# A last projection turned over: token blocks stationary, 512 output channels moving, and a LayerNorm that follows the tokens

## The chip, the cores and the metric

One core of one Trainium2 chip runs the program. The metric is the device time of the whole kernel in microseconds; lower is better. TensorE multiplies a stationary 128 x 128 block by columns that move past it, VectorE (DVE), ScalarE (ACT) and GpSimd (POOL) work on rows of 128 partitions, SyncE (SP) issues most transfers. The engines run on their own and meet at semaphores.

## What is computed

Two layers over T = 384 tokens (128 context, 256 latent) of D = 2048 channels. The second, odd layer is the one that matters here:

```python
def odd_mixer(h, w_in, conv_w, conv_b, ln_g, ln_b, w_out):
    a, b, g = jnp.split(h @ w_in, 3, axis=-1)
    u = a * jax.nn.sigmoid(b)
    u = dwconv(u, conv_w) + conv_b
    u = jax.nn.silu(layernorm(u, ln_g, ln_b))
    return (u * jax.nn.silu(g)) @ w_out
...
        y_p = layernorm(ALPHA * y_p + gt_c * o_p, ln_g[l], ln_b[l])
        y_s = layernorm(ALPHA * y_s + gt_s * o_s, ln_g[l], ln_b[l])
```

The input of w_out has 4096 channels (KE = 32 blocks of 128), its output 2048 (KD = 16 blocks). The gate gt is a vector over channels, one for context and one for latent tokens.

## The kernel before

Everything lies with channels on the partitions and the 384 tokens in the free dimension. Float32 accuracy comes from three products: each operand is split into a high part (fp32r) and the remainder, and high x high, high x low and low x high are added up in PSUM. The weights come as slabs of 8 blocks of 128 x 128 (512 KB): SP loads a slab into one of four raw buffers, ScalarE copies it to w_hi, and VectorE (even slabs) or GpSimd (odd slabs) subtracts to w_lo. Rings of four slabs tie the engines together: w_hi of slab k + 4 waits for slab k to be used. Engines work in order and by hand-written program: a "pair" is two slabs.

The phases follow each other: FIRST and EVEN (the even layer's input projection with attention), OUT0 (its output projection), ODD (the odd layer's input projection, 192 slabs or 96 pairs, with the convolution on VectorE), OUT1 (the last output projection, 4 bodies of 16 slabs), and the final LayerNorm with the stores.

In OUT1 a body makes four strips of 128 output channels x 384 tokens, one in each of the banks 0 to 3; a slab serves one strip. The weight block is stationary and the 384 tokens of o_hi or o_lo move. As each strip ends, VectorE multiplies it by the gate (a scalar for each partition) and adds it to the scaled x, less a pivot; ScalarE squares it, GpSimd adds up sum and squares over the blocks. Behind the last matmul `token_moments` sums over the partitions with ones on TensorE, VectorE and ScalarE make mean and root, TensorE spreads them, and `normalise_output` centres, scales and (with ScalarE's `affine`) applies gain and bias, block by block; SP stores 16 blocks of 192 KB.

In the last steps of ODD and the first of OUT1 the mixed activations o are still being made (NORM and SPLIT in `odd_step`: VectorE subtracts and scales, ScalarE applies SiLU, GpSimd multiplies by the gate path, ScalarE and VectorE split into o_hi and o_lo). ScalarE's `gate_out` evicts the last gate strips of ODD from the banks 2 and 3 at the start of its OUT1 part. The bank waits of TensorE and of ScalarE's eviction are these:

```python
                if t0 == 0:
                    if q == 0 and not (ph is FIRST and s in (CG_, XIN_)):
                        pe.wait_ge(bank_free[b], value)
                    pe.wait_ge(lo_ready[odd], ready)
...
                        if first and layer and not pair:
                            for s, (_, c) in odd_ready(PAIRS_ODD):
                                gate_out(s, c)
```

## Time and profile before

| | us |
|---|---|
| time, median of 3 runs | 2566.84 (2565.62 to 2566.97) |
| span of the profiled execution | 2565.9 |
| TensorE busy in it | 2515.2 |
| VectorE, ScalarE, GpSimd busy | 1959.0, 934.7, 922.9 |

The time is that of unprofiled runs. The profile has one execution of its own, whose span runs from the first to the last instruction; what lies around the span is not in it. Matmul records overlap: a matmul of 384 columns has a record of some 334 ns, and the next one starts much earlier. What a matmul costs in a stream is read from start to start.

### The profile page before, as it was taken

To read this page: it belongs to the slowest core of one execution; us is meant where nothing else is said; L and a number is where in the kernel's file an instruction comes from. 1 tells how busy PE (TensorE), PEld (TensorE's weight loads), DVE (VectorE), ACT (ScalarE), POOL (GpSimd) and SP (SyncE) were. 2 spreads that over 40 slices of the span, in tenths; PEclk is the share of its full clock that TensorE was granted. 3 is DMA by queue.
4 is the path that set the end of the run, shared out by engine and by line. 5 is a ranking of instruction groups with operands and counts; after the bars stand their busy time and mean duration, and the time that the engine had idled before them with its cause. 6 is when DMAs were issued, how large, how long until landed. Compare 5 with 4: busy or idle time off the path is not lost.

```text
span 2565.9 us, 40433 instructions
## 1 busy us (share of the span) xinstructions
PE 2515.2 (98%) x14486; PEld 2467.1 (96%) x14486; DVE 1959.0 (76%) x3411; ACT 934.7 (36%) x1232; POOL 922.9 (36%) x618
## 2 busy tenths in 40 slices
PE   6999999999999999999999999999999999999997
PEld 3699999999999999999999999999999999999997
DVE  2488888989888888889643389999999999484213
ACT  1233333333333333334322354333333333463223
POOL 0111111110111111111344566666666666572444
PEclk9999999999999999999999999999999999999998
DMA  9975666555565556565444334444343443564332
GB/s 387 347 214 189 200 193 198 184 195 197 193 209 195 191 184 199 189 200 161 155 147 139 129 111 136 138 138 130 126 137 129 135 129 130 180 208 131 124 125 89
DMA packets 131567, 442.02 MB, mean 172 GB/s; under 512 B 16720, under 2 KB 27216, under 8 KB 131456
## 3 DMA queue, kind: packets, MB, share of 16 engines
q1 hardware_dynamic: 114912, 409.23, 46.8%
q0 software_dynamic: 7328, 18.71, 3.6%
q10 hardware_dynamic: 9216, 12.59, 1.5%
q8 instruction: 70, 1.15, 0.2%
q14 instruction: 41, 0.34, 0.0%
HBM read 423.03 MB, written 15.18 MB: 171 GB/s over the span
## 4 chain that ended last, share of the span: by engine, by line
PE 90%; DVE 5%; DMA 3%; issue 1%; ACT 1%; POOL 1%; SPq 0%; ACTq 0%; DVEq 0%; POOLq 0%
PE bank L508 29%; PE bank L510 29%; PE bank L509 29%; DMA map<-in_w_ada_dram 2%; DVE w_lo L404 1%; PE bank L607 1%; PE bank L524 1%; DMA raw<-in_w_ada_dram 1%; DVE vk L1127 1%; DVE x L1317 0%; DVE part L1032 0%; ACT w_hi L725 0%; DVE o_lo L1176 0%; POOL w_lo L404 0%; DVE probT L1149 0%
## 5 line engine op out<-in xcount | busy, mean ns | idle before, releaser
L508 PE MATMUL bank<-h_hi,w_hi 128*128 128x384 f32 x3543 | 1191.9, 336 | 4.9 <-DVE h_lo L970 2.3
L510 PE MATMUL bank<-h_hi,w_lo 128*128 128x384 f32 x3543 | 1184.6, 334 | 0.0
L509 PE MATMUL bank<-h_lo,w_hi 128*128 128x384 f32 x3543 | 1184.3, 334 | 0.0
L725 ACT ACTIVATE w_hi<-raw 128x1024 fp32r<-128x1024 f32 x572 | 595.4, 1058 | 867.7 <-PE bank L510 611.4
L404 POOL TENSOR_TENSOR w_lo<-raw,w_hi 128x1024 fp32r<-128x1024 f32 x247 | 603.8, 2462 | 544.6 <-ACT w_hi L725 542.3
L508 PEld LDWEIGHTS bank<-h_hi,w_hi 128*128 128x128 f32 x3543 | 665.6, 188 | 22.8 <-issue 12.6
L509 PEld LDWEIGHTS bank<-h_lo,w_hi 128*128 128x128 f32 x3543 | 665.7, 188 | 0.6
L510 PEld LDWEIGHTS bank<-h_hi,w_lo 128*128 128x128 f32 x3543 | 665.5, 188 | 0.0
L404 DVE TENSOR_TENSOR w_lo<-raw,w_hi 128x1024 fp32r<-128x1024 f32 x325 | 396.4, 1236 | 257.9 <-ACT w_hi L725 244.8
L1393 DVE SCALAR_TENSOR_TENSOR bank<-up,cw,bank 128x399 f32<-128x399 f32 x896 | 487.0, 627 | 0.0
L508 PE MATMUL bank<-o_hi,w_hi 128*128 128x384 f32 x1024 | 343.1, 335 | 1.7 <-DVE w_lo L404 1.0
L510 PE MATMUL bank<-o_hi,w_lo 128*128 128x384 f32 x1024 | 342.1, 334 | 0.0
L509 PE MATMUL bank<-o_lo,w_hi 128*128 128x384 f32 x1024 | 342.1, 334 | 0.0
L1032 DVE SCALAR_TENSOR_TENSOR part<-raw,cond,part 128x512 f32<-128x512 f32 x450 | 309.3, 748 | 38.0 <-DMA raw<-in_w_ada_dram 38.0
L508 PEld LDWEIGHTS bank<-o_hi,w_hi 128*128 128x128 f32 x1024 | 192.2, 188 | 3.3 <-DVE w_lo L404 1.4
L509 PEld LDWEIGHTS bank<-o_lo,w_hi 128*128 128x128 f32 x1024 | 192.3, 188 | 0.3
L510 PEld LDWEIGHTS bank<-o_hi,w_lo 128*128 128x128 f32 x1024 | 192.2, 188 | 0.0
L1482 POOL DMA_DIRECT2D part<-part x30 | 25.1, 836 | 335.1 <-DVE part L1032 239.9
L1492 POOL DMA_DIRECT2D out_new_v_dram<-vk x16 | 9.2, 576 | 325.3 <-DVE k_lo L1111 325.3
L1241 DVE SCALAR_TENSOR_TENSOR x<-bank,mod,x 128x256 f32<-128x256 f32 x64 | 23.8, 413 | 110.8 <-PE bank L510 110.8
L1149 DVE STREAM_TRANSPOSE probT<-prob 32x224 f32<-32x224 f32 x256 | 103.2, 403 | 3.8
L1390 DVE SCALAR_TENSOR_TENSOR bank<-up,cw,pivot 128x128 f32<-128x128 f32 x64 | 102.5, 1645 | 0.0
(188 smaller groups left out, 1526.5 us busy)
## 6 DMA issues: line engine op xcount, KB each, us to landing
raw<-in_w_in_even_dram SPq DMA_DIRECT2D x256, 512.0 KB, 4.2
raw<-in_w_in_odd_dram SPq DMA_DIRECT2D x192, 512.0 KB, 3.3
raw<-in_w_ada_dram SPq DMA_DIRECT2D x120, 512.0 KB, 4.2
map<-in_w_ada_dram SPq DMA_DIRECT2D x64, 512.0 KB, 13.5
raw<-in_w_out_even_dram SPq DMA_DIRECT2D x64, 512.0 KB, 3.9
raw<-in_w_out_odd_dram SPq DMA_DIRECT2D x64, 512.0 KB, 3.3
gates<-sg ACTq DMA_DIRECT2D x32, 192.0 KB, 1.9
lg<-gates ACTq DMA_DIRECT2D x32, 192.0 KB, 3.8
```

Of the source, the lines that this page charges most:

```text
L404: eng.tensor_tensor(w_lo[mine][:], raw[slot][:], w_hi[mine][:].bitcast(F32), ALU.subtract)\
L508: pe.matmul(out, w_hi[slot][:, t, :], hi[:, kk, :], start=(kk == 0), stop=False)
L509: pe.matmul(out, w_hi[slot][:, t, :], lo[:, kk, :], start=False, stop=False)
L510: mm = pe.matmul(out, w_lo[slot][:, t, :], hi[:, kk, :], start=False, stop=last)
L524: mm = pe.matmul(bank[B_S1][32 * g:32 * g + 32, 0:CHUNK], cond[:, kk, :], maps[n % MAP_RING][:, g % 2, :], start=(q == 0), stop=(q == PART ...
L607: mm = pe.matmul(bank[B_V][:, TC:T].rearrange("p (a b) -> p a b", a=2), v, probT[:, j:j + 4:3, :], start=(j == 0), stop=(j == 2))
L725: act.activation(w_hi[mine][:], raw[slot][:], ACT.Copy).then_inc(hi_ready, 1)
L1032: ins = dve.scalar_tensor_tensor(to, w, by, to, ALU.mult, ALU.add)
L1127: ins = dve.transpose(vk[t:t + 32, :, c:c + 32], values[c:c + 32, :, t:t + 32])
L1149: ins = dve.transpose(probT[k:k + 32, :, q:q + 32], tiles[q:q + 32, :, k:k + 32])
L1390: ins = dve.scalar_tensor_tensor(a[:, a0 + z:b0 + z], src[:, a0 + z:b0 + z], wt, pivot[:, a0:b0], ALU.mult, ALU.subtract)
L1393: ins = dve.scalar_tensor_tensor(a, src, wt, a, ALU.mult, ALU.add)
```

## The change

The last output projection swaps its operands. A block of 128 tokens of o_hi or o_lo is stationary, and 512 output channels of w_hi or w_lo move past it; a body makes the three token tiles of 128 x 512 of a chunk of 512 channels, in the banks 0, 1, 2 or 3, 5, 6 in turn. A slab now holds two blocks of 128 input channels (halves) x 512 outputs. For each half the three products follow each other, each going over the three token tiles. Only the last four slabs of the last body run tile by tile, so that tile 0 is complete before tile 1. x itself must lie with tokens on the partitions: in ODD, TensorE transposes it block by block and ScalarE copies it back scaled by ALPHA. The gate becomes a row over channels, which needs two small transfers of the gate from SBUF to DRAM and a broadcast back; gain and bias come as broadcast rows too. The final LayerNorm uses bn_stats for each chunk and tile, and SP stores twelve pieces of 256 KB in the output's own layout. The pivot, the sums and squares of this layer and the former tail go.

```diff
+TILE_BANKS = ((0, 1, 2), (3, 5, 6))
+BY_TILE = OUT1.nw - RING
...
+        def tile_chunk(i, n):
+            return x[:, 4 * i:4 * i + 4, n * P:(n + 1) * P]
...
-                for r, (_, s, _) in enumerate(OUT1.order):
-                    load(OUT1, i, r, slab_of(OUT1, r, w_out_odd, i * 4 + s))
...
-                sp.dma_start(yT[:, t, :], x[:, t, :]).then_inc(y_stored, 16)
...
+                for r in range(OUT1.nraw):
+                    load(OUT1, i, r, w_out_odd[ds(i, 1), r].rearrange("s p f -> (s p) f"))
+            for n in range(TILES):
+                for i in range(OUT1.bodies):
+                    if i < SHIFTED_BY_DVE:
+                        sp.wait_ge(applied, n * SHIFTED_BY_DVE + i + 1)
+                    else:
+                        sp.wait_ge(applied_last, n + 1)
+                    sp.dma_start(y[n * P:(n + 1) * P, i * WIDE:(i + 1) * WIDE].rearrange("p (a b) -> p a b", b=P),
+                                 tile_chunk(i, n)).then_inc(y_stored, 16)
...
-                token_moments(2 * layer, x, KD * layer)
+                token_moments(0, x, 0)
+            def turn_input(t):
+                pe.wait_ge(x_ready, t + 1)
+                if t:
+                    pe.wait_ge(x_turned, t)
+                for n in range(TILES):
+                    ins = pe.transpose(bank[B_S0][:, n * P:(n + 1) * P], x[:, t, n * P:(n + 1) * P], eye)
+                ins.then_inc(x_tiles_ready, 1)
+            def tile_term(i, k, half, n, term):
+                c = 2 * k + half
+                out, slot = bank[TILE_BANKS[i % 2][n]], OUT1.w(0, k) % RING
+                high, low = (w[slot][:].rearrange("p t n -> p (t n)")[:, half * WIDE:(half + 1) * WIDE] for w in (w_hi, w_lo))
+                mine = slice(n * P, (n + 1) * P)
+                by, mixed = ((high, o_hi), (low, o_hi), (high, o_lo))[term]
+                return pe.matmul(out[:], mixed[:, c, mine], by, start=(c == 0 and term == 0), stop=(c == KE - 1 and term == 2))
+            def tile_step(i, k, half, n):
+                for term in range(3):
+                    mm = tile_term(i, k, half, n, term)
+                return mm
+            def tile_projection():
+                for i in range(OUT1.bodies):
+                    if i == 0:
+                        for b in TILE_BANKS[0]:
+                            pe.wait_ge(bank_free[b], OUT1.bank(0, b)[1])
+                    elif i == 1:
+                        pe.wait_ge(bank_free[3], OUT1.bank(0, 3)[1])
+                    else:
+                        pe.wait_ge(chunk_ready, TILES * (i - 1))
+                    last = i == OUT1.bodies - 1
+                    for k in range(BY_TILE if last else OUT1.nw):
+                        odd, ready = OUT1.low(i, k)
+                        pe.wait_ge(lo_ready[odd], ready)
+                        for half in range(2):
+                            if i == 0:
+                                pe.wait_ge(osplit_ready, KE + 2 * k + half + 1)
+                            for term in range(3):
+                                for n in range(TILES):
+                                    mm = tile_term(i, k, half, n, term)
+                                    if k == OUT1.nw - 1 and half and term == 2 and n < TILES - 1:
+                                        mm.then_inc(tile_done, 1)
+                        mm.then_inc(slab_used, 1)
+                for n in range(TILES):
+                    for k in range(BY_TILE, OUT1.nw):
+                        if not n:
+                            odd, ready = OUT1.low(OUT1.bodies - 1, k)
+                            pe.wait_ge(lo_ready[odd], ready)
+                        for half in range(2):
+                            mm = tile_step(OUT1.bodies - 1, k, half, n)
+                    mm.then_inc(tile_done, 1)
...
+                if k % 2 and 0 <= k // 2 - 4 < KD:
+                    turn_input(k // 2 - 4)
...
+            def tile_projection():
...
+                        if not (i == OUT1.bodies - 1 and pair == 7):
+                            split_high(OUT1, i, pair + 1)
+                        if i == 0:
+                            odd_step(PAIRS_ODD + pair)
+                            if pair == 3:
+                                for e in range(2):
+                                    act.wait_ge(gates_stored[e], 16 * (KE // 2 + 1))
+                                act.dma_start(g_row[:], ln_rows[0:1, :].partition_broadcast(P)).then_inc(g_row_landed, 16)
+                            if pair == 7:
+                                act.wait_ge(mixed_ready, KE)
+                                act.dma_start(b_row[:], ln_rows[1:2, :].partition_broadcast(P)).then_inc(b_row_landed, 16)
+                act.wait_ge(eps_ready, 1)
+                act.activation(eps_root[:], eps[:], ACT.Sqrt)
+                for n in range(TILES):
+                    act.wait_ge(var_known, n + 1)
+                    act.activation(deviation[:, n:n + 1], tile_mean_var[:, n, 1:2], ACT.Sqrt, bias=eps[:])\
+                       .then_inc(deviation_known, 1)
+                    act.wait_ge(shift_known, n + 1)
+                    chunk = tile_chunk(SHIFTED_BY_DVE, n)
+                    act.activation(chunk, chunk, ACT.Identity, bias=shift_tile[:, n:n + 1],
+                                   scale=rstd_tile[:, n:n + 1]).then_inc(scaled_out, 1)
...
+                if 5 <= n < KD + 5:
+                    act.wait_ge(x_tiles_ready, n - 4)
+                    act.activation(x[:, n - 5, :], bank[B_S0][:, 0:T], ACT.Copy, scale=ALPHA).then_inc(x_turned, 1)
+                if n == 2:
+                    act.wait_ge(gate_known, 1)
+                    for c in range(2):
+                        act.dma_start(gate_line[c].rearrange("(t p) -> p t", p=P), mod[:, 5, :, c], allow_slow_non_contiguous=True)\
+                           .then_inc(gate_stored, 16)
...
+                    act.wait_ge(rstd_ready, 2)
+                    act.wait_ge(gate_stored, 32)
+                    act.dma_start(gate_rows[:], gate_line.rearrange("(o c) d -> o c d", o=1).partition_broadcast(P))\
+                       .then_inc(gate_rows_landed, 16)
...
+                def gated(i, n):
+                    if i < OUT1.bodies - 1 and n == TILES - 1:
+                        dve.wait_ge(slab_used, OUT1.w(i, OUT1.nw - 1) + 1 + RING)
                     else:
...
+                        dve.wait_ge(tile_done, (TILES - 1) * i + n + 1)
+                    made_tile = bank[TILE_BANKS[i % 2][n]][:]
+                    dve.tensor_tensor(made_tile, made_tile, gate_rows[:, min(n, 1), i * WIDE:(i + 1) * WIDE], ALU.mult)\
+                       .then_inc(tile_gated, 1)
+                    dve.wait_ge(tile_gated, TILES * i + n + 1)
+                    chunk = tile_chunk(i, n)
+                    dve.tensor_tensor(chunk, chunk, made_tile.rearrange("p (a b) -> p a b", b=P), ALU.add)\
+                       .then_inc(chunk_ready, 1)
+                    dve.wait_ge(chunk_ready, TILES * i + n + 1)
+                    dve.bn_stats(chunk_stats[:, n, 6 * i:6 * i + 6], chunk).then_inc(chunk_counted, 1)
+                def normalised(n):
+                    dve.wait_ge(chunk_counted, TILES * (OUT1.bodies - 1) + n + 1)
+                    dve.bn_aggr(tile_mean_var[:, n, :], chunk_stats[:, n, :]).then_inc(var_known, 1)
+                    dve.wait_ge(deviation_known, n + 1)
+                    dve.reciprocal(rstd_tile[:, n:n + 1], deviation[:, n:n + 1]).then_inc(rstd_tile_ready, 1)
+                    dve.wait_ge(rstd_tile_ready, n + 1)
+                    dve.scalar_tensor_tensor(shift_tile[:, n:n + 1], tile_mean_var[:, n, 0:1], -1.0,
+                                             rstd_tile[:, n:n + 1], ALU.mult, ALU.mult).then_inc(shift_known, 1)
+                    dve.wait_ge(shift_known, n + 1)
+                    if not n:
+                        dve.wait_ge(b_row_landed, 16)
+                    for i in range(SHIFTED_BY_DVE):
+                        dve.scalar_tensor_tensor(bank[TILE_BANKS[0][i]][:], g_row[:, i * WIDE:(i + 1) * WIDE],
+                                                 shift_tile[:, n:n + 1], b_row[:, i * WIDE:(i + 1) * WIDE],
+                                                 ALU.mult, ALU.add).then_inc(shifted, 1)
+                    for i in range(SHIFTED_BY_DVE):
+                        dve.wait_ge(shifted, n * SHIFTED_BY_DVE + i + 1)
+                        dve.wait_ge(chunk_weighted, TILES * i + n + 1)
+                        chunk = tile_chunk(i, n)
+                        dve.scalar_tensor_tensor(chunk, chunk, rstd_tile[:, n:n + 1], bank[TILE_BANKS[0][i]][:]
+                                                 .rearrange("p (a b) -> p a b", b=P), ALU.mult, ALU.add).then_inc(applied, 1)
+                    dve.wait_ge(applied, (n + 1) * SHIFTED_BY_DVE)
...
+                for i in range(OUT1.bodies):
+                    for pair in range(8):
+                        if not (i == OUT1.bodies - 1 and pair == 7):
+                            split_low(OUT1, i, pair + 1)
+                        if i == 0:
+                            odd_step(PAIRS_ODD + pair)
+                        elif pair < TILES:
+                            if i == 1 and not pair:
+                                dve.wait_ge(gate_rows_landed, 16)
+                                dve.wait_ge(x_turned, KD)
+                            gated(i - 1, pair)
+                for n in range(TILES):
+                    gated(OUT1.bodies - 1, n)
+                    normalised(n)
...
+                def weighted(i, n, done, count):
+                    chunk = tile_chunk(i, n)
+                    pool.tensor_tensor(chunk, chunk, row_chunk(g_row, i), ALU.mult).then_inc(done, 1)
+                    pool.wait_ge(done, count)
+                for i in range(OUT1.bodies):
+                    for pair in range(8):
+                        if not (i == OUT1.bodies - 1 and pair == 7):
+                            low_half(pool, OUT1, i, 2 * pair + 3)
+                        if i == 0:
+                            odd_step(PAIRS_ODD + pair)
+                        elif 2 <= pair < 2 + TILES:
+                            if i == 1 and pair == 2:
+                                pool.wait_ge(g_row_landed, 16)
+                            pool.wait_ge(chunk_counted, TILES * (i - 1) + pair - 1)
+                            weighted(i - 1, pair - 2, chunk_weighted, TILES * (i - 1) + pair - 1)
+                pool.wait_ge(b_row_landed, 16)
+                for n in range(TILES):
+                    pool.wait_ge(scaled_out, n + 1)
+                    weighted(SHIFTED_BY_DVE, n, weighted_last, n + 1)
+                    chunk = tile_chunk(SHIFTED_BY_DVE, n)
+                    pool.tensor_tensor(chunk, chunk, row_chunk(b_row, SHIFTED_BY_DVE), ALU.add).then_inc(applied_last, 1)
...
+    a["w_out_odd"] = a["w_out_odd"][0].reshape(OUT1.nw, 2, P, OUT1.bodies, WIDE).transpose(3, 0, 2, 1, 4)\
+        .reshape(OUT1.bodies, OUT1.nw, P, SLAB_K * P)
```

How the change moves instructions, at the three places of which the prediction speaks. First TensorE at the end of the program, before: the last products of a strip (matmul lines name the output, then the moving and the stationary tile), then sums over the partitions (L631) and the spreading of mean and root (L637).

```order
8562 L508 MATMUL bank<-o_hi,w_hi 128x384
8563 L509 MATMUL bank<-o_lo,w_hi 128x384
8564 L510 MATMUL bank<-o_hi,w_lo 128x384
8565 L631 MATMUL bank<-ones,total 128x1 x3
8566 L631 MATMUL bank<-ones,energy 128x1 x3
8567 L631 MATMUL bank<-ones,x 128x1 x3
8568 L631 MATMUL bank<-ones,square_78 128x1 x3
8569 L637 MATMUL bank<-eye,rstd 128x128 x6
```

After, in the last body, with the numbers of banks and slots: one product goes to the banks 3, 5 and 6, then the next product.

```order
7370 L673 MATMUL bank3<-w_lo1,o_hi_51 128x512
7371 L673 MATMUL bank5<-w_lo1,o_hi_51 128x512
7372 L673 MATMUL bank6<-w_lo1,o_hi_51 128x512
7373 L673 MATMUL bank3<-w_hi1,o_lo_53 128x512
7374 L673 MATMUL bank5<-w_hi1,o_lo_53 128x512
7375 L673 MATMUL bank6<-w_hi1,o_lo_53 128x512
7376 L673 MATMUL bank3<-w_hi2,o_hi_51 128x512
```

The operands have changed sides and the width is 512; nothing is left for TensorE behind the last matmul. Next VectorE, after, from the completion of a token tile at the end of the program; these rows stand there once for each of the three tiles.

```order
902 L1461 TENSOR_TENSOR bank<-bank,gate_rows 128x512
903 L1465 TENSOR_TENSOR x<-x,bank 128x4x128
904 L1468 BN_STATS chunk_stats<-x 128x6
905 L1473 BN_AGGR tile_mean_var<-chunk_stats 128x2
906 L1475 RECIPROCAL rstd_tile<-deviation 128x1
907 L1477 SCALAR_TENSOR_TENSOR shift_tile<-tile_mean_var,rstd_tile 128x1
908 L1483 SCALAR_TENSOR_TENSOR bank<-g_row,shift_tile,b_row 128x512 x3
909 L1490 SCALAR_TENSOR_TENSOR x<-x,rstd_tile,bank 128x4x128 x3
```

They stand in the place of the centring and scaling of 16 blocks. Last, ScalarE, after, at the start of ODD: behind the split of slabs 6 and 7 it issues the two transfers of the gate, and the split of slabs 8 and 9 comes at the end of the piece.

```order
182 L811 ACTIVATE w_hi<-raw 128x1024 x2
183 L1023 DMA gate_line<-mod 128x16x1 x2
184 L982 ACT_TABLE_LOAD
185 L982 ACTIVATE sig_98<-bank 128x384
186 L972 ACT_TABLE_LOAD
187 L972 ACTIVATE sg_100<-bank 128x384
188 L974 DMA gates<-sg_100 128x384
189 L811 ACTIVATE w_hi<-raw 128x1024 x2
```

Before, the row of the two transfers is not there and the others are the same.

## Rows read from the trace of the kernel before

**Rows 1.** The page's first line

```profile
span 2565.9 us, 40433 instructions
```

**Rows 2.** Windows: busy of PE, PEld, DVE, ACT, POOL, then clock, DMA, GB/s

```profile
1500.00:2000.00 500.00, 500.00 (x2885) 499.73 (x2884) 483.30 (x859) 196.44 (x228) 334.23 (x165) 1.00 0.40 133
```

**Rows 3.** Timeline, last body: start, busy, engine, line, operation, [idle before]

```profile
2538.14 0.74 DVE L1241 SCALAR_TENSOR_TENSOR x<-bank,mod,x 128x256 f32<-128x256 f32 x2 [3.42 <-PE bank L510]
...
2542.30 0.74 DVE L1241 SCALAR_TENSOR_TENSOR x<-bank,mod,x 128x256 f32<-128x256 f32 x2 [3.42 <-PE bank L510]
```

**Rows 4.** Timeline of PE, opening of the odd layer, six matmuls apart

```profile
1475.16 0.33 PE L688 MATMUL bank<-h_hi,w_hi 128*128 128x384 f32 x1
...
1476.20 0.68 PE L693 MATMUL bank<-h_lo,w_hi 128*128 128x384 f32 x3
```

**Rows 5.** Timeline of PE, fp32 matmuls of two widths

```profile
1192.58 1.03 PE L607 MATMUL bank<-probT,vk 128*128 128x256 f32 x4
1193.44 0.59 PE L607 MATMUL bank<-probT,cv 128*128 128x256 f32 x2
...
2204.21 0.81 PE L661 MATMUL bank<-energy,ones 128*128 128x384 f32 x2
2204.85 0.81 PE L667 MATMUL bank<-o,ones 128*128 128x384 f32 x2
```

**Rows 6.** Timeline of PE around eight transposes

```profile
1445.56 0.34 PE L510 MATMUL bank<-o_hi,w_lo 128*128 128x384 f32 x1
1445.73 1.04 PE L564 MATMUL bank<-eye,part_late 128*128 128x128 f32 x8
1446.52 0.42 PE L508 MATMUL bank<-o_hi,w_hi 128*128 128x384 f32 x1
...
1447.14 0.33 PE L508 MATMUL bank<-o_hi,w_hi 128*128 128x384 f32 x1
```

**Rows 7.** Timeline of PE around the pivot sum of the second body

```profile
2358.22 0.34 PE L510 MATMUL bank<-o_hi,w_lo 128*128 128x384 f32 x1
...
2360.45 0.33 PE L510 MATMUL bank<-o_hi,w_lo 128*128 128x384 f32 x1
```

**Rows 8.** Timeline of ACT, then of PE, where the last projection begins

```profile
2280.29 0.49 ACT L866 ACTIVATE sg<-bank 128x384 f32<-128x384 f32 x1 [0.63 <-POOL o L1537]
...
2278.16 0.33 PE L508 MATMUL bank<-o_hi,w_hi 128*128 128x384 f32 x1
...
2283.51 0.33 PE L508 MATMUL bank<-o_hi,w_hi 128*128 128x384 f32 x1
```

**Rows 9.** Timeline of ACT and POOL around slab 8 of the odd layer

```profile
1503.77 0.34 ACTq L868 DMA_DIRECT2D gates<-sg  x1
...
1505.36 4.79 POOL L404 TENSOR_TENSOR w_lo<-raw,w_hi 128x1024 fp32r<-128x1024 f32 x2 [2.75 <-ACT w_hi L725]
...
1508.43 1.06 ACT L725 ACTIVATE w_hi<-raw 128x1024 fp32r<-128x1024 f32 x1 [0.65 <-PE bank L510]
```

**Rows 10.** Timeline behind the last matmul of the stream

```profile
2546.27 0.72 PE L631 MATMUL bank<-ones,total 128*128 128x1 f32 x6
...
2549.52 0.20 ACT L840 ACTIVATE rstd<-rstd 128x3 f32<-128x3 f32 x1 [1.75 <-DVE rstd L1306]
...
2551.40 0.71 ACT L844 ACTIVATE x<-x,par 128x384 f32<-128x384 f32 x1 [1.68 <-DVE x L1317]
...
2561.42 0.48 DVE L1363 TENSOR_SCALAR x<-x,par 128x384 f32<-128x384 f32 x1
```

**Rows 11.** A line's instructions: duration ns min/median/max, first and last start

```profile
L1317 DVE TENSOR_TENSOR x<-x,bank x32: 540/544/554, 1467.4 to 2560.8; 128x384 f32<-128x384 f32 x32
...
L1390 DVE SCALAR_TENSOR_TENSOR bank<-up,cw,pivot x64: 349/2191/2631, 1503.3 to 2174.6; 128x128 f32<-128x128 f32 x32, 128x256 f32<-128x256 f32 x32
...
L1593 POOL TENSOR_TENSOR x<-x,pivot x10: 987/991/1108, 2550.1 to 2558.8; 128x384 f32<-128x384 f32 x10
```

**Rows 12.** Transfers: queue, operation, count, KB each, median us to landing

```profile
out_yT_dram<-x SPq DMA_DIRECT2D x16, 192.0 KB, 2.0
```

More of the change, by code:

```diff
@@ L187 @@
 POOLED = KD - 1
[L188 to L195 removed]
+CALLS = (POOLED, KE - 2)
+BEFORE = (0, KD)
+CLEARED = (1, 2 + POOLED)
 class Steps:
@@ L1212, in body @@
                                 ada_bias((2, 5))
-                        if not layer and i == ph.bodies - 1 and pair == 6:
+                        if i == ph.bodies - 1 and pair == 6:
                             sum_late()
@@ L1368, in _ @@
+            out_projection(OUT0)
             dve.wait_ge(kv_stored, 32 * HEADS)
@@ L1544, in body @@
                             low_half(pool, ph, i, 2 * pair + 3)
-                        if first and layer:
-                            odd_step(PAIRS_ODD + pair)
                         for t in ADDED.get((i, pair), ()):
                             if t < POOLED:
-                                add_with_square(2 * layer, t, x, z_ready, KD * layer)
-                        if ends and not last:
+                                add_with_square(0, t, x, z_ready, 0)
+                        if ends:
```

180 lines of the change are left out of this document (77 added, 103 removed).

## The prediction

> **What bounds the kernel now.** I read the page first, for the span [rows 1], then the busy time by stretches, to see which engine has no idle time. Between 1500 and 2000 us TensorE is busy 500.00 of 500.00 us at a granted clock of 1.00, its 2.4 GHz level, and VectorE 483.30 [rows 2]. So a microsecond added to TensorE there is a microsecond of span; one added to ScalarE or GpSimd is free until it makes TensorE wait. The same holds in the last projection: the evictions of two successive strips start 4.16 us apart [rows 3], which is 24 matmuls at 0.1733 us with no gap. Only behind the last matmul do the other engines set the time. The reader is to see two clocks: the matmul stream until 2546.27, and 19.63 us of normalisation and stores behind it (2565.9 less 2546.27) [rows 1, 10].
>
> **The stream.** 1536 matmuls of 384 columns become 1152 of 512, and both are 589,824 columns, so only what a matmul costs beside its columns can be saved. 384 columns at 2.4 GHz are 160.0 ns, which leaves 13.3 ns of the 173.3. No matmul of this type with another width is in the trace. The nearest rows are fp32 ones, each issued as two records of two passes: 384 wide they start 0.64 us apart for two records, or 0.32 each (320 by columns), and 256 wide 0.86 us for four, or 0.215 each (213 by columns) [rows 5]. The remainder, about 2 ns, is the same at both widths, so it belongs to the instruction and not to the columns. I carry that over: 213.3 + 13.3 = 226.7 ns. Before 1536 x 0.1733 = 266.2 us, after 1152 x 0.2267 = 261.1, so **-5.1 us**. Bounds: if the 13.3 ns grow with the columns, 231.1 ns and nothing is saved; if they shrink to the 2.2 ns of the fp32 rows, 215.5 ns and 18.0 are saved. That each matmul now writes another bank than the one before costs nothing: in the opening of the odd layer the bank changes after two matmuls, and six of them take 1.04 us, again 0.1733 each [rows 4].
>
> [...]
>
> **The input turned.** x must now lie with tokens on the partitions: 16 times three 128 x 128 transposes, put into the odd layer's stream at the end of pairs 4 to 19. Eight such transposes stand in the trace: from the matmul before them to the fourth matmul start after it 1.58 us pass [rows 6], of which four slots of 0.1733 are matmuls; 0.89 us remain, 0.11 each with the change to and fro. For three I take 0.39 us (0.10 each and 0.09 for the change), **+6.2 us** for 16; bounds 5.3 (three eighths of 0.89) and 10.3 (0.215 each, the 256-wide row). ScalarE copies each turned block back, some 0.7 us in an 8.3 us pair, with the next transposes a whole pair away: no wait.
>
> The sum over x[:, 0] and ones in the second body goes: from 2358.22 to 2360.45 there are nine slots (1.56 us) and this sum, so **-0.7 us** [rows 7].
>
> **The opening of the projection.** Two waits change places here. Now the first slab wants mixed blocks 0 to 7 within 4.16 us and takes 5.35 (2278.16 to 2283.51) [rows 8]: 1.19 us of waiting for o_lo, which goes, since the new slab 0 wants blocks 0 and 1 only. But the first matmuls now go to banks 0, 1 and 2, where slab 0 went to bank 0 alone. Bank 2 holds a gate strip of the odd layer, which ScalarE only evicts at 2280.29 for 0.49 us, because its normalisation steps come first [rows 8]. TensorE reached the projection at 2278.16, so it waits 2.6 us, with the whole projection queued behind. Net **+1.4 us** (bounds -1.2, if ScalarE comes in time, and +2.4, if it must also have evicted bank 3, another 0.95).
>
> **The tail.** Before, 19.63 us. After, the last four slabs run token tile by token tile, 24 matmuls or 5.44 us each, so tile 0 is complete 10.88 us before the end E of the stream and VectorE starts on it 0.2 us later. What VectorE does per tile, from 384-wide rows of 0.54 us [rows 11] plus 128 columns at 0.96 GHz (0.13): times gate, plus x, statistics, each waiting for the one before, 3 x 0.71 = 2.1; aggregate, root on ScalarE (0.20 [rows 10]), reciprocal, shift, each with its hand-over, 0.85; three shift rows and three applications at 0.60 us apart, 3.7. That is 6.7 us. To it comes a block. The shift operation reads g_row and b_row, two SBUF operands. The one row of that form in the odd layer takes 349 ns at best and 2191 in the median, whereas the form with one operand in PSUM never exceeds 554 [rows 11]; the former queues behind a GpSimd operation under way. Here ScalarE's chunk (0.70 us at 384 [rows 10], so 0.8) releases GpSimd 0.9 us after the shift is known, and GpSimd's multiply of 1.3 us (0.99 at 384 [rows 11]) stands in front of the third shift row: +1.0. So 7.7 us a tile, 23.1 for three, more than the 10.9 us of cover: VectorE ends at E - 10.9 + 0.2 + 23.1 = E + 12.4. From VectorE's last instruction to the end of the span there are 4.0 us now (2561.90 to 2565.9) [rows 1, 10]; the last four stores are 256 KB instead of 192, which landed in 2.0 us [rows 12], and come close together: I add 0.8. Tail 17.2 instead of 19.6, **-2.4 us** (bounds -5.4 without the block, and 0 with 0.09 us more on each of the nine large operations of a tile).
>
> GpSimd's gain multiplications and the split of the weights lie in bodies 1 to 3, under a stream that leaves GpSimd mostly idle; they cost nothing there. The broadcasts of the gate, gain and bias rows (2, 1 and 1 MB) fall between weight loads whose slot is free about two pairs before it is wanted.
>
> **Sum.** -5.1 + 6.2 - 0.7 + 1.4 - 2.4 = -0.6 us. The profiled span of 2565.9 becomes 2565.3. The median of the runs is 2566.84, 0.9 above the span, so I forecast **2566.3 us**.
>
> **The rivals.**
> Stream cheaper than thought: the 13.3 ns might be a weight load that shows behind 160 ns and is hidden behind 213. For it: no longer matmul of this type stands in the trace. Against it: each of the eight transposes loads its own block too, and they start 0.10 us apart (1445.73 to 1446.52) [rows 6], so a load fits into 0.17 as it does into 0.23. It gives 2566.3 - 1152 x 0.0112 = 2553.4. Chance 0.10.
> Stream by columns: 231.1 ns, 2566.3 + 5.1 = 2571.4. Chance 0.10.
> Tail or opening better: no GpSimd operation in front of the shifts (-3.0), or also bank 2 free in time (-2.6): 2563.3 or 2560.7. Chance 0.16.
> Slower, by ScalarE's queue: ahead of the split of slab 8 ScalarE now issues two transfers of the gate whose elements are 4 bytes apart from their neighbours, 128 x 16 each. Slab 8's low half is ready at 1507.8 (half of GpSimd's 4.79 us from 1505.36), and TensorE turns to it at 1508.43: 0.7 us of cover [rows 9]. A transfer of 128 rows holds ScalarE 0.34 us [rows 9], and two at that price use the cover up and no more. If the hold grows with the pieces, 16 x 0.34 = 5.4 each, TensorE waits 10.9 - 0.7 = 10.2 us and the time is 2576.5. It decides for slower from 3.2 us a transfer. For the gate rows themselves there are 700 us. Chance 0.08.
> The Trainium skill (DMA: Bandwidth & Descriptors, section Rules for kernel authors) says that a strided last dimension becomes one descriptor per element, here 2048 in each of the two transfers. No run before shows how long issuing such a transfer holds ScalarE.
> My forecast holds 0.50, on its own 2563 to 2570; 0.06 is for what I have not seen.
>
> **How the numbers follow.** What this kernel's measurement can tell from no change is 0.2%, 5.1 us: faster is below 2561.7, slower above 2572.0. Faster: the cheap stream 0.10, the better end of tail and opening 0.08, half of the unseen 0.03, and 0.03 for my case with two terms too high: 0.24. Slower: ScalarE's queue 0.08, half of the by-columns case, 0.05, dear transposes (10.3 instead of 6.2, 2570.4) with any other miss 0.04, unseen 0.03: 0.20. The range of 2560.5 to 2572.0 leaves the cheap stream below and the queue above.
>
> **What the profile after will show.** Matmuls of 512 columns start 0.227 us apart; 0.216 or 0.231 decide for a rival. Turning costs TensorE 0.39 us a time. TensorE waits some 2.6 us for ScalarE before its first 512-wide matmul and hardly in the odd layer; a gap of several us near 1510 is the queue. VectorE runs without idle time from 10.7 us before the stream's end, the third shift row of each tile being the long one, and the span ends 17 us behind the stream. I am wrong if the matmul price is off by 5 ns, since each ns is 1.15 us.

## The result

The changed kernel takes 2574.42 us (median of 6 runs, 2571.88 to 2576.41) and the kernel before 2566.9 us in the runs beside it: ratio 1.0024, 95% interval 1.0014 to 1.0035. It is slower, by 7.5 us, where 2566.3 was forecast; the range to 2572.0 misses it too. The profiled execution took 2571.88 us, the quickest of the six, and its span is 4.4 us longer than the one before; the account at the end says where the rest of the 7.5 is.

The first line of the page after, then windows (busy of TensorE, its weight loads, VectorE, ScalarE, GpSimd, then clock, DMA share, GB/s):

```profile
span 2570.3 us, 39590 instructions
```

```profile
1500.00:1510.00 10.00, 8.63 (x49) 8.17 (x48) 8.26 (x17) 6.89 (x8) 5.21 (x3) 1.00 0.59 11
1510.00:1520.00 10.00, 10.00 (x61) 9.97 (x60) 9.96 (x21) 0.92 (x1) 2.86 (x2) 1.00 0.90 120
1520.00:1530.00 10.00, 8.59 (x51) 8.27 (x50) 7.43 (x9) 8.37 (x12) 8.80 (x4) 1.00 0.62 217
1500.00:2000.00 500.00, 497.22 (x2881) 495.67 (x2880) 477.14 (x843) 199.13 (x239) 326.21 (x161) 1.00 0.41 131
...
2280.00:2300.00 20.00, 17.50 (x79) 15.03 (x78) 19.28 (x28) 15.87 (x27) 15.42 (x12) 0.91 0.63 207
...
2400.00:2500.00 100.00, 100.00 (x443) 82.84 (x442) 25.70 (x28) 26.55 (x25) 32.55 (x15) 1.00 0.40 130
```

Against [rows 2], TensorE no longer works without a gap in the odd layer: 2.78 us are missing between 1500 and 2000, all of them before 1530. In the first of these windows the DMA engines are busy 0.59 of the time and move 11 GB/s. That is the thing to see: busy and moving next to nothing. Over 1495 to 1520 the view of transfers has these lines for the kernel after (queue, packets, MB, share; then issues with KB each and median us to landing):

```profile
q1 hardware_dynamic: 439, 1.63, 56.4%
q10 hardware_dynamic: 4272, 0.21, 13.2%
...
raw<-in_w_in_odd_dram SPq DMA_DIRECT2D x4, 512.0 KB, 12.5
gates<-sg ACTq DMA_DIRECT2D x1, 192.0 KB, 16.1
gate_line<-mod ACTq DMA_DIRECT2D x2, 8.0 KB, 16.8
```

and this one for the kernel before, over the same stretch:

```profile
raw<-in_w_in_odd_dram SPq DMA_DIRECT2D x6, 512.0 KB, 3.3
```

Two transfers of 8 KB take 16.8 us in the median, and the weight loads of 512 KB beside them 12.5 instead of 3.3. The timeline of ScalarE and its queue in the same stretch, and TensorE's two waits in it:

```profile
1497.48 2.28 ACTq L1023 DMA_DIRECT2D gate_line<-mod  x2
...
1503.41 1.13 ACTq L974 DMA_DIRECT2D gates<-sg  x1
...
1519.08 1.06 ACT L811 ACTIVATE w_hi<-raw 128x1024 fp32r<-128x1024 f32 x1 [10.88 <-DMA raw<-in_w_in_odd_dram]
```

```profile
1508.20 0.45 PE L536 MATMUL bank<-h_hi,w_hi 128*128 128x384 f32 x1 [1.37 <-POOL w_lo L430]
...
1522.73 0.41 PE L536 MATMUL bank<-h_hi,w_hi 128*128 128x384 f32 x1 [1.41 <-POOL w_lo L430]
```

There are two gaps, with two causes. The first, at 1508.20, is the hold of ScalarE's queue: the two issues hold it for 2.28 us together and the next one for 1.13 instead of 0.34, so that its splits from 1504.64 on, and GpSimd's low half of slab 8 behind them (1505.78 instead of 1505.36), are 1.9 us late, counted from the start of the odd layer, which is 1.48 us earlier here. The second, at 1522.73, is the loads: the high half that ran at 1508.43 before [rows 9] runs at 1519.08, having waited 10.88 us for a raw load. GpSimd's low half comes behind it, and TensorE waits for that.

In this execution the odd layer costs 8.8 us more (from its first matmul to the last before the projection, 1469.64 to 2278.16 before, 1468.16 to 2285.46 after): 5.3 for the transposes (below) and 3.5 for the two gaps and the slower starts around them. The opening of the projection, after:

```profile
2285.28 0.34 PE L538 MATMUL bank<-h_hi,w_lo 128*128 128x384 f32 x1
...
2287.42 0.49 ACT L972 ACTIVATE sg<-bank 128x384 f32<-128x384 f32 x1 [0.62 <-POOL o L1678]
...
2288.12 1.62 PE L673 MATMUL bank<-w_hi,o_hi 128*128 128x512 f32 x3 [2.50 <-DVE o_lo L1290]
2289.53 1.48 PE L673 MATMUL bank<-w_lo,o_hi 128*128 128x512 f32 x3
2290.81 1.10 PE L673 MATMUL bank<-w_hi,o_lo 128*128 128x512 f32 x3
2291.75 0.85 PE L673 MATMUL bank<-w_hi,o_hi 128*128 128x512 f32 x3
```

TensorE is free at 2285.46, ScalarE empties bank 2 until 2287.91, and the projection starts at 2288.12: a wait of 2.66 us. (The row names o_lo, but the blocks that are wanted first were split by 2279.4; the kernel with other banks, below, has no such wait.) Then three matmuls take 1.41, 1.28 and 0.94 us where 0.68 is the rule later on. 1.28 for three is 0.427 each, which is what 512 columns come to at 1.2 GHz: after the wait TensorE ran for some 3 us at the lower level, and that is 1.6 us more. The clock of 0.91 in the window is the same thing seen from outside.

The tail, after (the end of the stream is at 2550.8, the end of the span at 2570.3):

```profile
2543.36 3.13 DVE L1483 SCALAR_TENSOR_TENSOR bank<-g_row,shift_tile,b_row 128x512 f32<-128x512 f32 x3
...
2544.32 1.61 POOL L1703 TENSOR_TENSOR x<-x,g_row 128x512 f32<-128x512 f32 x1 [6.01 <-ACT x L934]
2546.01 1.62 POOL L1722 TENSOR_TENSOR x<-x,b_row 128x512 f32<-128x512 f32 x1
2546.40 2.05 DVE L1490 SCALAR_TENSOR_TENSOR x<-x,rstd_tile,bank 128x512 f32<-128x512 f32 x3
...
2548.49 0.70 DVE L1461 TENSOR_TENSOR bank<-bank,gate_rows 128x512 f32<-128x512 f32 x1
...
2556.78 0.70 DVE L1461 TENSOR_TENSOR bank<-bank,gate_rows 128x512 f32<-128x512 f32 x1
...
2562.99 2.05 DVE L1490 SCALAR_TENSOR_TENSOR x<-x,rstd_tile,bank 128x512 f32<-128x512 f32 x3
```

VectorE takes 8.29 us a tile (2548.49 to 2556.78) and ends at 2565.04, 5.3 us before the span does. The tail is 19.5 us, against 19.63 before.

### The profile page after: what moved, and what is told of

Same layout as the page of the kernel before. It is cut to its first block, busy times and chain, and to the rows that moved or that the text cites. A ratio compares the mean times of both kernels' runs of the same rounds, so it can differ in the third digit from the quotient of the medians.

```text
span 2570.3 us, 39590 instructions
## 1 busy us (share of the span) xinstructions
PE 2513.5 (98%) x14118; PEld 2419.2 (94%) x14118; DVE 1966.7 (77%) x3391; ACT 929.8 (36%) x1224; POOL 897.2 (35%) x592
## 4 chain that ended last, share of the span: by engine, by line
PE 89%; DVE 4%; DMA 3%; issue 1%; ACT 1%; POOL 1%; SPq 0%; ACTq 0%; DVEq 0%; POOLq 0%
PE bank L536 26%; PE bank L537 25%; PE bank L538 25%; PE bank L673 10%; DMA map<-in_w_ada_dram 2%; DVE w_lo L430 1%; PE bank L635 1%; PE bank L552 1%; DMA raw<-in_w_in_odd_dram 1%; DMA raw<-in_w_ada_dram 1%; ACT w_hi L811 0%; POOL w_lo L430 0%; DVE vk L1241 0%; DVE o_lo L1290 0%; DVE part L1146 0%
## 5 line engine op out<-in xcount | busy, mean ns | idle before, releaser
L430 POOL TENSOR_TENSOR w_lo<-raw,w_hi 128x1024 fp32r<-128x1024 f32 x247 | 596.7, 2432 | 571.3 <-ACT w_hi L811 569.1
L536 PE MATMUL bank<-o_hi,w_hi 128*128 128x384 f32 x512 | 171.6, 335 | 1.3 <-DVE w_lo L430 1.0
L538 PE MATMUL bank<-o_hi,w_lo 128*128 128x384 f32 x512 | 171.1, 334 | 0.0
L537 PE MATMUL bank<-o_lo,w_hi 128*128 128x384 f32 x512 | 171.0, 334 | 0.0
L673 PE MATMUL bank<-w_hi,o_hi 128*128 128x512 f32 x384 | 111.2, 391 | 2.5 <-DVE o_lo L1290 2.5
L673 PE MATMUL bank<-w_lo,o_hi 128*128 128x512 f32 x384 | 111.1, 391 | 0.0
L673 PE MATMUL bank<-w_hi,o_lo 128*128 128x512 f32 x384 | 110.7, 390 | 0.0
L536 PEld LDWEIGHTS bank<-o_hi,w_hi 128*128 128x128 f32 x512 | 96.1, 188 | 2.1 <-DVE w_lo L430 1.4
```

Of the source, the lines that this page charges most:

```text
L430: eng.tensor_tensor(w_lo[mine][:], raw[slot][:], w_hi[mine][:].bitcast(F32), ALU.subtract)\
L536: pe.matmul(out, w_hi[slot][:, t, :], hi[:, kk, :], start=(kk == 0), stop=False)
L537: pe.matmul(out, w_hi[slot][:, t, :], lo[:, kk, :], start=False, stop=False)
L538: mm = pe.matmul(out, w_lo[slot][:, t, :], hi[:, kk, :], start=False, stop=last)
L673: return pe.matmul(out[:], mixed[:, c, mine], by, start=(c == 0 and term == 0), stop=(c == KE - 1 and term == 2))
```

## The experiments

Eleven kernels, each timed beside the kernel before. The last column is the difference of the medians in the same series; the changed kernel's is +7.5. The intervals reach some 2.5 us to either side, so a difference of 1 to 3 us between two of these kernels is not shown by the medians alone and rests on the traces.

| kernel | median us | ratio to before, 95% | less before |
|---|---|---|---|
| before + the two transfers | 2573.98 | 1.0026 (1.0015 to 1.0036) | +7.0 |
| after, without them | 2568.85 | 1.0006 (0.9997 to 1.0015) | +1.9 |
| after, other banks | 2571.60 | 1.0013 (1.0004 to 1.0022) | +4.7 |
| after, without transposes | 2570.15 | 1.0010 (1.0001 to 1.0019) | +3.2 |
| after, block by block | 2574.22 | 1.0026 (1.0016 to 1.0035) | +7.2 |
| after, gate turned by TensorE | 2569.45 | 1.0004 (0.9995 to 1.0013) | +2.4 |
| after, bias row in banks | 2573.07 | 1.0021 (1.0011 to 1.0030) | +6.1 |
| after, gate turned + banks + bias row | 2562.97 | 0.9981 (0.9972 to 0.9990) | -4.1 |
| after, one transfer | 2569.76 | 1.0005 (0.9995 to 1.0014) | +2.2 |
| after, transfers at pair 40 | 2568.49 | 1.0003 (0.9994 to 1.0012) | +0.9 |
| after, transfers by GpSimd | 2574.36 | 1.0027 (1.0017 to 1.0037) | +6.8 |

**The transfers alone.** The kernel before, with these lines of the change added:

```diff
+                if n == 2:
+                    act.wait_ge(gate_known, 1)
+                    for c in range(2):
+                        act.dma_start(gate_line[c].rearrange("(t p) -> p t", p=P), mod[:, 5, :, c], ...)
```

> The kernel before, with one part of the change alone: ScalarE issues the two transfers of the gate (128 x 16 elements each, 4 bytes apart from their neighbours) in the third pair of the odd layer, and waits for them 600 us later; nothing reads them. Theory A (the transfers of single elements take the DMA engines from the weight loads while they last, some 15 us, so that the split of two slabs comes late and TensorE waits): a gap of TensorE of 3 to 5 us between 1500 and 1525, ScalarE's high halves waiting for raw loads, time 2570 to 2573. Rival B (only the hold of ScalarE's queue counts, 0.4 and 1.8 us less the cover of 0.7): +1.5, 2568.4, with no wait for raw loads. Rival C (the transfers are free, and the odd layer is longer by the transposes alone): 2566.9.

It costs 7.0 us, nearly the whole loss of the change, and more than expected. Its windows:

```profile
1510.00:1520.00 10.00, 10.00 (x60) 10.00 (x59) 9.97 (x21) 0.00 (x0) 2.70 (x2) 1.00 0.89 77
1520.00:1530.00 10.00, 7.04 (x32) 6.75 (x31) 6.48 (x7) 7.01 (x9) 7.69 (x4) 0.83 0.70 250
...
1500.00:2000.00 500.00, 496.25 (x2850) 495.37 (x2850) 477.81 (x848) 195.55 (x226) 328.77 (x162) 1.00 0.42 131
```

ScalarE does nothing at all between 1510 and 1520; it waits for raw loads. 3.75 us of TensorE are missing, in a gap of 0.79 us at 1508.05 and one of 2.96 at 1523.79, and from 1520 to 1530 the granted clock is 0.83: behind the longer gap TensorE runs at the lower level, as behind the opening's wait. Theory A stands, with the time 1 us above its range; what it left out is that second cost.

**Without the transfers.** The same lines taken out of the changed kernel.

> The changed kernel without the two transfers of single elements; the gate rows are filled from the gain and bias rows in their place, with the same broadcast, so the output is not the reference's. Theory A (weight loads starved): the waits for raw loads and for GpSimd's low half near 1508 and 1523 go, and 4 to 7 us with them: 2567.5 to 2570.5. Rival B (hold of the queue alone): 1.5 less, 2573. Rival C (free): 2574.4.

5.6 us less, and TensorE has its whole stretch back:

```profile
1500.00:2000.00 500.00, 500.00 (x2901) 499.19 (x2900) 478.73 (x848) 201.23 (x242) 329.08 (x162) 1.00 0.40 131
```

From the odd layer's first matmul (1468.98) to the last projection's first (2285.45) pass 816.5 us, of which 2.7 are the opening's wait; before it was 808.5. So 5.3 us are left for the 48 transposes.

**Other banks.**

```diff
-TILE_BANKS = ((0, 1, 2), (3, 5, 6))
+TILE_BANKS = ((0, 5, 6), (1, 2, 3))
```

> The changed kernel with other banks: the first body of the projection accumulates in banks 0, 5 and 6 (5 and 6 were last read hundreds of us before), the next in 1, 2 and 3. Theory A (TensorE waits 2.66 us for ScalarE to empty bank 2, and the wait lets the granted clock fall, which costs 1.6 us more): the wait goes, the first groups of three start 0.68 us apart, the clock in 2280:2300 is 1.00 and not 0.91; 4.3 less, 2570.1. Rival B (the clock falls there for another reason): the wait alone goes, 2571.8, clock still 0.91. Rival C (another wait is right behind it, for the low halves of the mixed blocks, as in the kernel before where it cost 1.2 us): 1.5 less, 2572.9.

2.8 us less, between A and C. The start is as theory A has it, and then comes a wait that was not there:

```profile
2288.19 0.86 PE L673 MATMUL bank<-w_hi,o_hi 128*128 128x512 f32 x3
2288.89 0.85 PE L673 MATMUL bank<-w_lo,o_hi 128*128 128x512 f32 x3
...
2306.81 0.98 PE L673 MATMUL bank<-w_hi,o_hi 128*128 128x512 f32 x3 [2.10 <-DVE w_lo L430]
```

The wait and the low clock are gone: 0.70 us lie between the first group and the second. Of the 4.3 us gained TensorE gives 2.3 back before 2306.81 (the group before starts at 2303.87 and needs 0.68), where it waits for a low half of the weights. VectorE and GpSimd before it:

```profile
2298.49 4.95 DVE L1291 TENSOR_TENSOR o_lo<-o,o_hi 128x384 fp32r<-128x384 f32 x4
2303.35 3.40 DVE L430 TENSOR_TENSOR w_lo<-raw,w_hi 128x1024 fp32r<-128x1024 f32 x1
```

```profile
2298.08 4.94 POOL L1679 TENSOR_TENSOR o<-o,lg 128x384 f32<-128x384 f32 x4
2302.97 2.70 POOL L430 TENSOR_TENSOR w_lo<-raw,w_hi 128x1024 fp32r<-128x1024 f32 x1
```

Four low halves of the mixed blocks take 4.95 us and a weight's low half 3.40, while GpSimd works beside them; the same two take 2.47 and 2.04 us in the changed kernel, at 2295.26 and 2297.66. There TensorE starts 2.7 us later against the odd layer's end, and no wait is seen. So rival C was right that another wait stands behind the first, and wrong on what for. That GpSimd's work makes VectorE late is read from the trace, not tried.

**Without the transposes.** The call of `turn_input` is left out.

> The changed kernel without the 48 transposes of the input; ScalarE copies x in place in their stead, so the output is not the reference's. Theory A (48 transposes cost TensorE 0.33 us for three, 5.3 in all, and nothing else): 2569.1. Rival B (they also cause the waits near 1508 and 1523, since they shift TensorE against the splits): those waits are gone too, 2565. Rival C (hidden in waits that were there anyway): over 2572.

4.3 us less, 1 us above A and so between A and C. The trace rules B out: with no transposes TensorE still misses 4.16 us between 1500 and 2000, with the clock at 0.83 in 1520:1530, a loss that the profiled execution of the changed kernel does not have. So the gap is not theirs, and their price is the 5.3 us above.

**Block by block.** The loop over the three token blocks outside the loop over the three products.

```diff
-                            for term in range(3):
-                                for n in range(TILES):
+                            for n in range(TILES):
+                                for term in range(3):
```

> The changed kernel with the loops turned inside out: each token block takes its three products in a row (one bank three times, one stationary block twice), then the next block. Theory A (a matmul of 512 columns takes its 226.7 ns whatever bank or block the one before had): 2574.4, groups of three still 0.68 us apart. Rival B (coming to the same bank again costs): each matmul 2 ns or more longer, 2577 or above. Rival C (the repeated stationary block makes it cheaper, since its load can be done without): two thirds of the loads as before, 2 ns less for each matmul or more, under 2572.

```profile
2400.00:2500.00 100.00, 100.00 (x442) 82.78 (x442) 24.84 (x27) 25.44 (x24) 34.65 (x16) 1.00 0.38 126
```

442 matmuls in 100 us, as with the change (443), and as many weight loads as matmuls. The order of products is worth nothing either way.

**The gate turned by TensorE.** Two transposes at pair 20 into a bank, one copy by ScalarE, one transfer of rows of 512 bytes:

```diff
+                    pe.transpose(bank[B_S0][0:KD, c * P:(c + 1) * P], mod[:, 5, :, c], eye)
...
+                    act.dma_start(gate_line.rearrange("c (t p) -> t c p", p=P),
+                                  gate_turned[0:KD, :].rearrange("t (c p) -> t c p", p=P))
```

> The changed kernel with the gate brought into row form in another way: TensorE turns it (two transposes 100 us later in the odd layer), ScalarE copies it out, and one transfer of 32 rows of 512 bytes takes the place of the 4096 single elements. Theory A (what cost 5.6 us was the number of pieces): 5.3 less than with the change, 2569.1, no wait for raw loads, and the transfer lands in under 4 us. Rival B (any transfer to this place does it): 2574.4, with a gap of TensorE where the new transfer is issued.

5.0 us less by the medians, with nothing left out of the computation, and TensorE busy 500.00 of 500.00 us between 1500 and 2000. The transfer lands in 1.4 us.

**The bias row in two banks.**

```diff
-                                                 shift_tile[:, n:n + 1], b_row[:, i * WIDE:(i + 1) * WIDE],
+                                                 shift_tile[:, n:n + 1],
+                                                 bank[BIAS_BANKS[i]][:] if i else b_row[:, 0:WIDE],
```

> The changed kernel with copies of the second and third chunk of the bias row in banks 4 and 7, which are free (ScalarE makes them in the second body), so that two of the three shift rows of a tile read one operand in SBUF and one in PSUM; the first runs before GpSimd has work. Theory A (each tile lost time because a VectorE operation with two SBUF operands queued behind GpSimd's two): the shift rows take 0.7 us each instead of 3.1 for the longest, a tile 5.9 instead of 8.3, the end comes 12.3 us behind the stream instead of 19.5: 2567.2. Rival B (GpSimd's share is the limit: its two operations and the stores behind them end last, or are themselves slowed by VectorE): tiles shorter, but the tail 15 us or more, 2570 to 2572. Rival C (the rows are long for another reason, so a bank changes nothing): 2574.4.

The expectation was wrong by its own reading: 3.13 us is the time of the three shift rows together, not of the longest (the third, 1.80). After the edit, in the same place:

```profile
2547.69 0.76 DVE L1491 SCALAR_TENSOR_TENSOR bank<-g_row,shift_tile,b_row 128x512 f32<-128x512 f32 x1
...
2548.36 1.40 DVE L1491 SCALAR_TENSOR_TENSOR bank<-g_row,shift_tile,bank 128x512 f32<-128x512 f32 x2
2548.65 1.30 POOL L1712 TENSOR_TENSOR x<-x,g_row 128x512 f32<-128x512 f32 x1 [6.00 <-ACT x L941]
```

The three take 2.0 us instead of 3.0 from the first to the operation behind them (2547.69 to 2549.68, 2543.36 to 2546.40), GpSimd's operation 1.30 instead of 1.61, a tile 7.28 instead of 8.29, and the tail is 16.7 us long. So theory A has the mechanism and not the size: it costs 1.0 us a tile, as the prediction said. Rival B has the length of the tail (15 us or more) but not the reason: GpSimd ends at 2565.74, before VectorE at 2566.29. The runs show 1.4 us less, the trace 2.7; the interval of the ratio, 1.0011 to 1.0030, holds both, and no gain too. The Trainium skill (SBUF — State Buffer, section SBUF: two separate sides) says that a VectorE operation with two inputs in SBUF and one of GpSimd that reads SBUF block each other for the whole instruction; this trace agrees, with 1.0 us gone once one input is in PSUM.

**All three.** The gate turned by TensorE, the other banks, the bias row in banks.

> The changed kernel with all three edits: the gate turned by TensorE, the first body in banks 0, 5 and 6, and the bias row in two banks for the tail. Theory A (three separate causes, so their gains add: 5.3, 2.8 and 7.2): 2559.1, 0.997 of the kernel before. Rival B (they share a cause, so that less than two thirds is seen): 2564 or above, no faster than before beyond 0.1%.

2562.97 us, ratio 0.9981 (0.9972 to 0.9990): faster than the kernel before by 4.1 us, and than the changed one by some 11.5. It misses A's 2559.1, whose third gain was the misread one; with 2.7 in its place A gives 2563.6, an account made after the run.

**One transfer.** Only one of the two is issued.

> The changed kernel with one of the two transfers of single elements (2048 pieces instead of 4096); the gate rows are filled from the gain and bias rows, so the output is not the reference's. Theory A (the weight loads starve for as long as pieces are being moved, and the four raw slots cover the first part of it): the loads are late by half as long, some 7 us instead of 15, which the slots ahead cover; no wait of TensorE for the low halves, 2568.9 to 2569.5. Rival B (a fixed cost for each such transfer): half of the 5.6 is left, 2571.6. Rival C (any element-wise transfer stalls the loads whatever its size): 2574.4.

Here, over 1495 to 1520:

```profile
raw<-in_w_in_odd_dram SPq DMA_DIRECT2D x6, 512.0 KB, 5.0
...
gate_line<-mod ACTq DMA_DIRECT2D x1, 8.0 KB, 11.1
```

ScalarE waits 5.1 us for a raw load instead of 10.9, and TensorE between 1500 and 2000 not at all. It is A, 0.3 us above its range: 2048 pieces fit into the cover, 4096 do not. This edit shortens the hold too (0.41 us, and 0.34 for the next issue); the last experiment parts the two.

**Later.** `n == 2` becomes `n == 40`.

> The changed kernel with the two transfers of single elements issued at pair 40 of the odd layer instead of pair 2, some 315 us later, in the steady stream. Theory A (loads starve wherever it happens, since they run ahead by the same four slots all along): the gap of TensorE moves to about 1815 to 1840 and the time stays, 2574.4. Rival B (pair 2 was a bad place, right behind the layer's opening where loads and splits are barely ahead; later the cover is larger): the gap is under 1 us, 2569 to 2570.5.

5.9 us less by the medians, 6.6 by the differences to the kernel before, with nothing else changed. Over 1800 to 1830, and in the windows:

```profile
raw<-in_w_in_odd_dram SPq DMA_DIRECT2D x7, 512.0 KB, 12.6
gate_line<-mod ACTq DMA_DIRECT2D x2, 8.0 KB, 15.8
```

```profile
1820.00:1830.00 10.00, 10.00 (x60) 10.00 (x59) 9.93 (x22) 4.08 (x5) 5.24 (x4) 1.00 0.79 27
```

The loads starve just as long (12.6 us), and the longest wait of ScalarE for one is 3.9 us instead of 10.9; TensorE has no gap. Theory A was wrong on the place and rival B right: behind the opening of the layer the loads are hardly ahead of the splits, 300 us later they are. The kernel without the transfers has the numbers: the load that the late split at pair 2 reads lands at 1505.66 and is read at 1507.52, 1.9 us later; the two that starve at pair 40 land there at 1819.29 and 1821.71 and are read 11.4 and 10.0 us later.

**By GpSimd.** The same transfers, same pair, another issuer.

> The changed kernel with the two transfers of single elements issued by GpSimd in the same pair instead of by ScalarE. Theory A (what costs is the moving of 4096 pieces by the DMA engines, whoever asks for it): raw loads still land late (12 us and not 3.3), ScalarE still waits for them near 1510, and the time is 2573 to 2576. Rival B (ScalarE's queue, held 0.4 and 1.8 us and then 1.1 for the next transfer, was the cost): 2569. Rival C (GpSimd is held while it makes the pieces, and its low halves come late in turn): ScalarE on time, TensorE waiting for GpSimd, 2572 or more.

```profile
raw<-in_w_in_odd_dram SPq DMA_DIRECT2D x6, 512.0 KB, 16.2
...
gate_line<-mod POOLq DMA_DIRECT2D x2, 8.0 KB, 18.7
```

```profile
1531.15 0.52 PE L663 MATMUL bank<-eye,x 128*128 128x128 f32 x3 [3.70 <-ACT x L1019]
```

The same time as with the change. ScalarE's next issue takes 0.35 us, so its queue is free, and TensorE has no gap near 1508. But the loads land in 16.2 us, ScalarE waits for one until 1526.86, its copy that the transposes want comes behind that, and TensorE waits 3.70 us. GpSimd waits for ScalarE in turn, so it is not rival C.

The hold is seen in the other traces, but the times do not show that it adds to the loss. In the six with both transfers issued by ScalarE at pair 2, its two issues and the next one take 2.0 to 3.7 us together, and the first gap grows with them, from 0.15 to 1.75 us. The second gap is mostly shorter where the first is longer (4.00 behind 0.16, 1.41 behind 1.37, but 2.53 behind 1.75); together they are 2.8 to 4.3 us, and 3.70 here with no hold. That a TensorE which was held up already has less to wait for the loads is read from these traces, not tried.

## Why the prediction was wrong

**The step that failed** is that the sum put the two transfers of the gate at nothing, by the sentence "two at that price use the cover up and no more". It and the rival behind it, "if the hold grows with the pieces" (chance 0.08), asked only how long the issue holds ScalarE. The two hold it 2.28 us, where 0.7 were expected or 10.9, and a gap of 1.37 us stands where the rival put its 10.2, at slab 8. But the time is as long without the hold, as the transfers by GpSimd show. That the measured 2574.4 lies near the rival's 2576.5 is chance. The cost is in the transfers' own time, for which the sum had no term: the text said that the loads' slots are "free about two pairs before" they are wanted, of the broadcasts, and did not ask what 4096 elements do to a load under way. The loads beside them land after 12.5 us instead of 3.3, and that costs 5.6 us (without the transfers) to 7.0 (the transfers alone). The Trainium skill (DMA: Bandwidth & Descriptors, section Rules for kernel authors) says that a strided last dimension is lowered to one descriptor per element; the trace agrees, with 4272 packets of 0.21 MB on that queue, where 1495 to 1520 had 144 before. The prediction drew only the length of the issue from it.

**Term by term**, by what was measured: stream -5.1 as forecast (three matmuls 0.68 us apart, 226.7 ns each, so neither of the two rivals on it; the stream of 262.7 us is 1152 x 0.2267 and the 1.6 of the low clock). The constant of 13.3 ns carried over from the narrower matmul held. The Trainium skill (TensorE: Matmul & The Clock Gate, section Back-to-back issue gap) gives N / 2.4 + 2.5 ns for a warm matmul taken by itself, an estimate of 215.8 ns here, and says that a stream with weight loads comes out lower at this width; this trace shows neither, and the measured 226.7 ns decides. Transposes +5.3 instead of +6.2: after a transposition four slots of 0.1733 and three transposes take 1.02 us, so 0.33 for three, the lower bound. The row by which one reads it:

```profile
1516.49 0.34 PE L538 MATMUL bank<-h_hi,w_lo 128*128 128x384 f32 x1
1516.66 0.49 PE L663 MATMUL bank<-eye,x 128*128 128x128 f32 x3
...
1517.51 0.33 PE L536 MATMUL bank<-h_hi,w_hi 128*128 128x384 f32 x1
```

Pivot sum -0.7, not taken apart. Opening +3.1 instead of +1.4, and this too is a term of the sum that was mis-sized: the wait is 2.66 us where 2.6 was forecast, but 1.6 us at half the clock follow, and no term had them. Tail -0.2 instead of -2.4: the block by GpSimd is the 1.0 us a tile that was forecast, the rest of a tile 7.3 and not 6.7. The shift rows and applications start 0.66 to 0.77 us apart (0.60 was taken), the small operations ahead of them take 1.02 (0.85 was taken) and the three large ones 2.19 (2.1 was taken), which is 0.6 of a tile and 1.8 of the tail; the last stores take 5.3 us and not 4.8. Together -5.1 - 0.7 + 5.3 + 3.1 - 0.2 = +2.4, and that is near what the four kernels without the transfers' cost show: +1.9, +2.4, +2.2 and +0.9. With 5.6 for the transfers it is 8.0, beside the 7.5 measured. In the profiled execution the two gaps took 3.5, which makes 5.9; the odd layer began 1.5 us earlier than in the one before, and 4.4 is the difference of the spans. The 0.9 us that the prediction added to the span is no constant of the kernel: other executions of the kernel before take 1.9 us more than their span, so the profiled one was 0.9 above the median.

In the profiled execution the loss was in two gaps of 1.37 and 1.41 us, and the clock stayed at 1.00. All five other traces with both transfers by ScalarE at pair 2 (the transfers alone, other banks, no transposes, block by block, bias row in banks) have a second gap of 2.5 to 4.0 us and show the clock at 0.83 from 1520 to 1530; their odd layer is 5.8 to 6.7 us longer than the same one without the transfers, gaps and clock together. That fits this execution being the quickest of its six; the other five have no trace.

## What to carry to other kernels

Price a transfer by its pieces and by what shares the DMA engines while it lasts, not by its bytes or by the issue alone: 16 KB in 4096 pieces took the loads beside them from 3.3 us to 12.5 and more, whichever engine asked. If its result is wanted late, issue it where the loads are well ahead, or turn the data on chip and send whole rows. And a wait of TensorE costs more than its length when the clock falls behind it (1.6 us here), so a new wait in a full stream should be given two prices.

## What the hardware showed that was not expected

A wait of 2.66 us was followed by about 3 us at 1.2 GHz. By the idle time in its row, the opening's wait was 2.5 to 3.1 us in seven of the traces (2.50 in the changed kernel's), and six of them ran at the lower level behind it; the seventh, with the transfers by GpSimd, waited 2.70 us and lost 0.1. Where the wait was 1.9 us (block by block) or 1.8 (gate turned by TensorE) 0.1 is lost too. So the length of the wait alone does not settle it.

From the first issue to the last landing 4096 elements took 19 to 22 us, some 5 ns each, and one transfer of 2048 took 11.1; in the first 10 us behind 1500 the engines moved 11 GB/s. Asked for by GpSimd the same elements appear as 96 packets and not some 4100, and take about as long: the count of packets does not tell the price. VectorE's low half of a weight, 1.23 us where nothing is beside it, took 3.40 when GpSimd did the same operation at the same time.
